# Second-layer attention of a two-layer decoder: new order of the query blocks, PSUM banks from a free list, one product on GpSimd, last head's maps turned on TensorE

## What is computed

```python
# layer 2, per head h (8 heads): two q/k maps of 128, values of 256
for i in range(S // 128):                       # 16 query blocks of 128 tokens, causal
    s = einsum('qmd,kmd->mqk', q[q0:kl], k[:kl]) * scale + bias   # m = 0, 1
    p = softmax(where(mask, s, -inf))
    a = p[0] - lam * p[1]                       # the attention map
    o = a @ v[:kl]                              # 128 x 256
o = o * rsqrt(mean(o*o) + eps) * subln_g        # RMSNorm gain, 256 values
y = (o * (1 - lambda_init) * silu(z)) @ w_out
x = LayerNorm(ALPHA * x + y)
```

## Time and profile before

| | us |
|---|---|
| median of 3 runs | 2826.72 (2821.49 to 3012.68) |
| profiled execution, its own time | 2812.25 |
| its span, slowest core (core 1) | 2810.7 |
| spans of the eight cores | 2795.7 to 2810.7 |
| PE busy in the span | 2586.8 (92%) |

### The profile page before, as it was taken

How to read it: one execution, slowest core, us unless ns; L and a number is a source line. 1 busy time by engine, 2 the same in 40 slices (tenths; PEclk the granted TensorE clock), 3 DMA queues, 4 the chain that set the end, 5 groups by cost and what they waited for, 6 DMA issues and landing times.

```text
span 2810.7 us, 70949 instructions; the slowest of 8 cores (2795.7 to 2810.7 us)
## 1 busy us (share of the span) xinstructions
PE 2586.8 (92%) x25016; PEld 1785.8 (64%) x25016; DVE 1549.8 (55%) x3656; ACT 1243.1 (44%) x3240; POOL 312.7 (11%) x645
## 2 busy tenths in 40 slices
PE   7899999999999999999999888989889898976998
PEld 4587777777777775443575648475657666663443
DVE  2544444444444443657566565656576557653766
ACT  0365555555555562533144443534353434433321
POOL 2000000000000000000112121211212122221100
PEclk9999999999999999999999999999999999998999
DMA  9222222222223269997434443444434344577753
GB/s 154 50 41 40 39 40 48 48 39 41 39 40 55 41 97 212 222 179 206 69 57 71 60 71 54 77 54 78 65 63 71 55 70 70 92 143 152 187 165 135
DMA packets 351435, 245.16 MB, mean 87 GB/s; under 512 B 279792, under 2 KB 295792, under 8 KB 346480
## 3 DMA queue, kind: packets, MB, share of 16 engines
q1 hardware_dynamic: 304736, 145.02, 23.6%
q0 software_dynamic: 45920, 92.45, 21.4%
q10 hardware_dynamic: 432, 3.15, 0.3%
HBM read 224.21 MB, written 49.15 MB: 97 GB/s over the span
## 4 chain that ended last, share of the span: by engine, by line
PE 75%; DMA 9%; DVE 8%; issue 5%; ACT 1%; SPq 1%; DVEq 0%; POOL 0%; another core or an unknown queue 0%; ACTq 0%; POOLq 0%
PE pb L525 23%; PE pb L510 23%; PE pb L338 12%; DMA M<-M 6%; PE pb L677 4%; PE pb L662 4%; PE pb L1115 4%; PE pb L1025 3%; DVE M L1089 1%; DMA A<-xs 1%; DMA x1d<-M 1%; DMA M<-x 1%; DVE M L1054 1%; DVE M L410 1%; SPq L857 1%
## 5 line engine op out<-in xcount | busy, mean ns | idle before, releaser
L665 ACT ACTIVATE M<-pb,M 128x256 bf16<-128x256 f32 (+1 forms) x1152 | 522.1, 461 | 411.0 <-PE pb L677 340.2
L525 PE MATMUL pb<-M,B 128*128 128x128 bf16 x7456 | 518.1, 222 | 0.0
L510 PE MATMUL pb<-B,M 128*128 128x512 bf16 x1848 | 505.6, 383 | 3.4 <-DVE M L773 3.3
L525 PEld LDWEIGHTS pb<-M,B 128*128 128x128 bf16 x7456 | 459.6, 99 | 16.1 <-issue 0.2
L525 PE MATMUL pb<-M,A 128*128 128x128 bf16 x6432 | 450.1, 220 | 17.3 <-DVE M L554 10.8
L510 PE MATMUL pb<-A,M 128*128 128x512 bf16 x1576 | 429.4, 386 | 5.8 <-DVE M L561 3.3
L525 PEld LDWEIGHTS pb<-M,A 128*128 128x128 bf16 x6432 | 392.5, 98 | 31.2 <-issue 19.5
L1115 PE MATMUL pb<-M 128*128 128x256 bf16 x1088 | 221.5, 288 | 114.7 <-DMA M<-M 85.4
L662 PE MATMUL pb<-M 128*128 128x256 bf16 (+1 forms) x1152 | 307.5, 267 | 8.8 <-ACT M L665 4.7
L677 PE MATMUL pb<-M 128*128 128x129 bf16 x2176 | 311.9, 221 | 1.7 <-DVE M L669 0.8
L536 DVE TENSOR_TENSOR M<-pb,M 128x512 f32<-128x512 f32 x248 | 171.1, 690 | 237.9 <-PE pb L510 99.0
(11 more groups left out here) (134 smaller groups left out, 2581.2 us busy)
## 6 DMA issues: line engine op xcount, KB each, us to landing
M<-w1s POOLq DMA_DIRECT2D x128, 256.0 KB, 5.1
M<-w0s POOLq DMA_DIRECT2D x30, 1024.0 KB, 10.4
M<-x SPq DMA_DIRECT2D x15, 1024.0 KB, 6.8
x1d<-M SPq DMA_DIRECT2D x30, 512.0 KB, 4.6
A<-x1d SPq DMA_DIRECT2D x15, 1024.0 KB, 5.3
y<-A SPq DMA_DIRECT2D x30, 512.0 KB, 3.3
gtd<-M SPq DMA_DIRECT2D x238, 64.0 KB, 2.1
B<-w1o POOLq DMA_DIRECT2D x4, 2048.0 KB, 32.4
```

The costliest lines, as they stand in the source:

```text
L510: ins = e.matmul(pb[b][:, :], lhsT=Ws.ap[:, kc * 128:kc * 128 + 128], rhs=Xs.ap[:, kc * 512:kc * 512 + 512], start=(first and kc == 0), st ...
L525: ins = e.matmul(pb[b][:, kk * 128:(kk + 1) * 128], lhsT=Xs.ap[:, kc * 512 + kk * 128:kc * 512 + kk * 128 + 128], rhs=Ws.ap[:, kc * 128:kc ...
L665: P.op("act", lambda e: e.activation(out=pt.ap[:, 0:w], in_=pb[s][:, 0:w], func=AF.Exp, bias=bs.ap[:, j * 8 + I:j * 8 + I + 1], scale=SCAL ...
```

## The change

1. Heads 0 to 5 take the query blocks in the order `MIX` (a late one, an early one, ...), with score steps due within five units less 3000 instead of six less 2000, and value steps from 7000 (was 4000) after the next unit's start. `PV_LAG` is 10000 (was 8500).
2. The accumulator bank is taken from a free list; it returns 1500 (was 1000) of emitted work after its last reader.
3. The product with the norm gain (L953 before) is issued on POOL.
4. The four DVE sums of a unit's weights are emitted 1500 apart, not together; the sums of x for the second half are placed differently in the first head.
5. `Blk.turn`: where `u == ND - 1`, the map is turned by PE matmuls against the identity into a score bank and copied back by ACT, up to eight 128x128 squares at a time, with no DMA; its values may start 3000 after.
6. In the last head the units run k0, k1, q0, q1, v0, z0, v1, z1 (the digit is the token half) instead of v0, v1, z0, z1 at the end; two of the output weights' DMAs, the first residual and two read-backs are issued at the start of v1 instead of z1 (the first read-back was at v0).
7. Residuals have eight buffers (was four), the read-back buffers move, blocks 0 to 3 are one step of the output projection, the LayerNorm rows are loaded from POOL's queue.

```diff
-                [V("A", k * 8192, 8192, F32) for k in range(3)]]
+                [V("A", 16384, 8192, F32), V("A", 40960, 8192, F32), V("M", oW + 1024, 8192, F32), V("M", oW + 18432, 8192, F32),
+                 V("A", 57344, 8192, F32), V("M", oS[0] + 8192, 8192, F32), V("M", oS[0], 8192, F32), V("M", oW + 10240, 8192, F32)]]
...
-        STEPS = [[[0, 1, 2], [3]]] * 2
+        STEPS = [[[0, 1, 2], [3]], [[0, 1, 2, 3]]]
...
-            for o, a, b in ((4, 1, 0), (1, 3, 1), (5, 3, 4), (6, 2, 5)):
-                sub_v(w[o], w[a], w[b], 0, ALU.subtract)
+            for q, (o, a, b) in enumerate(((4, 1, 0), (1, 3, 1), (5, 3, 4), (6, 2, 5))):
+                wpend[n].append(lambda o=o, a=a, b=b: sub_v(w[o], w[a], w[b], 0, ALU.subtract))
+                sc.after(1500 * q if n > 3 else 0, lambda: wpend[n].pop(0)() if wpend[n] else None)
...
-                    P.op("dve", lambda e: e.tensor_tensor(out=z3[:, st * 4:st * 4 + 4, m * 128:(m + 1) * 128], in0=b4(H.ap),
+                    P.op("pool", lambda e: e.tensor_tensor(out=z3[:, st * 4:st * 4 + 4, m * 128:(m + 1) * 128], in0=b4(H.ap),
...
                 self.t = V("M", self.p.off + 2 * w, 2 * w)
+                self.half = False
+                if u == ND - 1:
+                    self.ready = None
+                    sc.after(4000, self.turn)
+                    return
                 key = self.no % NAT
...
+            def turn(self):
+                for c in range(0, self.i + 1, 8):
+                    s, n = s_bank(), min(8, self.i + 1 - c)
+                    def f(e, s=s, n=n, c=c):
+                        for j in range(n):
+                            ins = e.transpose(pbh[s][:, j * 128:(j + 1) * 128], self.p.ap[:, (c + j) * 128:(c + j + 1) * 128], ident.ap)
+                        return ins
+                    P.op("pe", f, reads=self.p.rr(c * 128, (c + n) * 128) + ident.r, writes=bank(s))
+                    P.op("act", lambda e, s=s, n=n, c=c: e.activation(out=self.t.ap[:, c * 128:(c + n) * 128], in_=pbh[s][:, 0:n * 128], func=AF.Copy),
+                         reads=bank(s), writes=self.t.rr(c * 128, (c + n) * 128))
+                self.drop()
+                self.ready = sc.t + 3000
...
-                    self.acc = 5 + cnt["ab"] % 2
-                    cnt["ab"] += 1
+                    self.acc = accs.popleft()
...
-                sc.after(1000, lambda: cnt.update(da=cnt["da"] - 1))
+                sc.after(1500, lambda: accs.append(B.acc))
...
-        PV_LAG = 8500
-        cnt.update(da=0, ab=0)
+        PV_LAG = 10000
+        accs = deque([5, 6])
...
+        MIX = [8, 15, 9, 14, 0, 13, 1, 12, 2, 11, 3, 10, 4, 7, 5, 6]
...
-                    order = P1 + P0 if u < ND - 2 else P0 + P1
-                    DT.add(u, order, at[n], at[n + 6] - 2000, at[n + 1] + 4000, at[n + 7] + 4000)
+                order = MIX if u < ND - 2 else P0 + P1
+                DT.add(u, order, at[n], at[n + 5] - 3000, at[n + 1] + 7000, at[n + 7] + 3000)
...
+            if (u, k, p) == (ND - 1, 2, 1):
+                G.insert(0, [call(load_gp, 0, 0, 14), call(load_wo, 1, 0), call(load_res, 1, 0), call(load_wo, 1, 1), call(load_gp, 1, 0, 14)])
```

More of the change, by code:

```diff
@@ L713, in tr @@
                     P.op("dve", lambda e: e.tensor_copy(out=t.ap[:, 15 * 256:4096], in_=pbh[s][:, 0:256]), reads=bank(s), writes=t.rr(15 * 256, 4096))
-                sc.after(1800, tr)
+                sc.after(3000, tr)
                 return
@@ L804, in epi_step @@
                 else:
-                    order += [(b, i) for b in blocks[2:] for i in (0, 1)] + [(b, i) for i in (2, 3) for b in blocks]
+                    order = [(b, i) for b in blocks for i in (0, 1)] + [(b, i) for i in (2, 3) for b in blocks]
             elif li == 0 and blocks[-1] == 15:
@@ L846, in scale @@
                         x1_tr(b)
-                    if hf == 1 and b + 3 < 16 and b:
-                        sc.after(5000 * li, lambda: load_res(li, b + 3))
+                    if hf == 1 and li == 0 and 0 < b < 13:
+                        load_res(0, b + 3)
+                    if hf == 1 and li == 1 and b < 8:
+                        sc.after(5000, lambda: load_res(1, b + 8))
             for n in range(4):
@@ L872, in build_program @@
         wun = [[] for _ in range(NW)]
+        wpend = [[] for _ in range(NW)]
         neglam = misc.ap[:, 5:6]
@@ L878, in build_program @@
         dg = [V("M", oG + 1024, 512), V("M", oG + 1536, 512), V("M", oP + 2560, 512)]
-        gp = [V("A", 49152, 8192)] + [V("A", 24576 + k * 8192, 8192) for k in range(3)]
+        gp = [V("A", k * 8192, 8192) for k in (0, 1, 3, 4)]
         def load_w1(n, extra=None):
@@ L1219, in start @@
                     b = self.blocks[0]
-                    if cnt["da"] < 2 and b.ready is not None and (force or b.ready <= sc.t):
+                    if accs and b.ready is not None and (force or b.ready <= sc.t):
                         self.blocks.popleft()
-                        cnt["da"] += 1
                         self.pv.extend((c, f, t) for (c, f), t in zip(b.pv, b.tp))
@@ L1358, in build_program @@
         for u in range(1, ND):
-            for k in range(4):
+            for k in range(4 if u < ND - 1 else 2):
                 ps = (0, 1) if u == ND - 1 or (u == ND - 2 and k == 3) else (1, 0)
                 seq += [(u, k, p) for p in ps]
+        seq += [(ND - 1, k, p) for p in range(2) for k in (2, 3)]
         ucost = lambda k: 56 * mm_ns(512) if k < 2 else 224 * mm_ns(128)
@@ L1391, in build_program @@
                 flow([call(bar_fin, u - 1, p)])
[L1392 to L1398 removed]
+            if k == 2 and second and u < ND - 1:
+                order = MIX if u < ND - 2 else P0 + P1
+                DT.add(u, order, at[n], at[n + 5] - 3000, at[n + 1] + 7000, at[n + 7] + 3000)
+            if (u, k, p) == (ND - 1, 2, 0):
+                DT.add(u, range(8), at[n], at[n + 1] + 4000, at[n + 1] + 5000, at[n + 3])
+                DT.add(u, range(8, 16), at[n + 1] + 4000, end + 10000, at[n + 3], end + 25000)
             G = unit(u, k, p)
@@ L1426, in build_program, with load_late @@
                 G.insert(0, [call(diff_E, u)])
-            if u == ND - 1:
-                if k == 2 and p == 0:
-                    G.insert(0, [call(load_gp, 0, 0, 14)])
-                if k == 3 and p == 1:
-                    G.insert(0, [call(load_wo, 1, 0)] + [call(load_res, 1, q) for q in range(3)] + [call(load_wo, 1, 1)])
+            if (u, k, p) == (ND - 1, 1, 1):
+                G.insert(0, [call(wfree.extend, [slot("A", 49152 + 2048 * q) for q in range(3)])])
+            if (u, k, p) == (ND - 1, 2, 0):
+                G.insert(3, [call(sum_w1, 4 * u + 3)])
+            if (u, k, p) == (ND - 1, 2, 1):
+                G.insert(0, [call(load_gp, 0, 0, 14), call(load_wo, 1, 0), call(load_res, 1, 0), call(load_wo, 1, 1), call(load_gp, 1, 0, 14)])
             flow(sum(G, []))
+        load_res(1, 1)
         load_wo(1, 2)
-        load_gp(1, 0, 14)
-        load_wo(1, 3)
-        for dt, f in ((7000, call(load_rows, 1, "act")), (10000, call(load_res, 1, 3, "act")),
+        for dt, f in ((4000, call(load_res, 1, 2)), (8000, call(load_wo, 1, 3)), (10000, call(load_res, 1, 3)), (16000, call(load_rows, 1, "pool")),
                       (24000, call(load_gp, 2, 0, 14)), (34000, call(load_gp, 3, 0, 14))):
             sc.after(dt, f[1])
-        for n, bl in enumerate(STEPS[0] + PAIRS):
+        late = [4, 5, 6, 7]
+        def load_late(force=False):
+            if not late:
+                return
+            if not all((ND - 1, i) in done_fin for i in range(16)):
+                assert not force
+                sc.after(2000, load_late)
+                return
+            while late:
+                load_res(1, late.pop(0))
+        sc.after(30000, load_late)
+        for n, bl in enumerate(STEPS[1] + PAIRS):
+            if n == 1:
+                flow([call(finish_g, 7), call(load_late, True)])
             for I in sorted({b // 2 for b in bl}):
@@ L1443, in build_program @@
             G = epi_step(1, bl, lambda I: gp[I % 4], lambda I: h7[I])
-            for I in (4 + n,) if n < 4 else ():
+            for I in ((4, 5), (6,), (7,))[n] if n < 3 else ():
                 G.append([(0.0, lambda I=I: load_gp(I, 0, 14))])
```

44 lines of the change are left out of this document (23 added, 21 removed).

## The result

The changed kernel took 0.957 of the time of before (95% interval 0.952 to 0.963). Some executions of every kernel here show a lower granted clock on the cores of one die or both and take longer; times and ratios are of the others alone. The profiled execution took 2700.41 us with a span of 2698.8, against 2812.25 and 2810.7: 111.9 us off the span, where the prediction had 85.7. The forecast was 2741 us with a range of 2700 to 2815; 0.957 x 2826.72 is 2705, near the lower end of that range.

A forecast was written before the change was run, and what follows sets the result against it. PE, busy 2586.8 of 2810.7 us, was taken as bound by waits for chains and slow clock. Terms 61 + 3 - 4.7 + 34 - 7.6 = 85.7 us off gave 2725, plus 16 made 2741 us; range 2700 to 2815.

The forecast's parts named there:

- Heads 0 to 5: New order, windows and lag there: 11 us off each of four heads, 8.5 off heads 0 and 5, 61 us together.
- DMA transposes: Middle heads: PE's waits for transposes, at blocks 15 and 12, fall from 10.7 to 3.5 us per head.
- Score banks: Middle heads: scores stand closer, so PE's waits for score banks rise from 2.7 to 4.2 us per head.
- Slow clock: Middle heads: with the long waits mostly gone, time lost to PE's low clock falls from 7.5 to 4.5 us per head.
- Product on POOL: Gain product, 64 instructions of 128x512: 0.7 us each, bounds 0.28 and 2; no gain booked, bounds -5 and +15 us.
- Turning: Head 7 and blocks 8 to 14 of head 6: 220 squares at 0.056 us add 12.3 us; tail waits fall by 34.
- Part 4 and head 6: Last head's order: output weights land in 32.4 us, covered, nothing booked; head 6 gains 3 us from the longer lag.
- A: Heads: lead doesn't matter, landings follow DMA load and the wait moves to another block; only tail gains, 2802 us; chance 0.15.
- B: Tail gains nothing: the 22.7 us wait comes back at the first output matmul; 2766 us; chance 0.11.
- C: DVE and POOL hinder each other at the 64 products, 15 to 30 us reaching PE; 2764 us; chance 0.13.
- D: Slower: in heads 0 to 5 transposes of blocks 8 to 15 all land late, +100 us, 2927 us; chance 0.08.
- E: The change does something unsaid: seven blocks of head 6 are turned too, 4.7 us, already in the sum; no chance given.

The follow-up runs named there:

- e4: The changed kernel with the gain product back on DVE instead of POOL, nothing else changed: ratio to before 0.961 (0.957 to 0.965).
- e2: The changed kernel with before's order of query blocks in heads 0 to 5, but the new windows and lag: ratio to before 0.974 (0.970 to 0.978).
- e8: The kernel before with only the new block order, windows and lag for heads 0 to 5: ratio to before 0.966 (0.963 to 0.969).
- e6: The changed kernel without any turning on PE, all those blocks transposed by SP's DMAs: ratio to before 0.970 (0.967 to 0.973).
- Part 1 alone: Same run as e8: new block order, windows and lag for heads 0 to 5 put into the kernel before: ratio 0.966.
- the rest of the change alone: The changed kernel with before's block order, windows and lag in heads 0 to 5: ratio to before 0.975 (0.972 to 0.978).

## Why the prediction was right

Its sign, its place and its range held; it was 26 us short on the span. The time is 36 us off, not 26, since I also added the 16 us by which before's median lies above its profiled span; the changed kernel's times, 2700.41 and 2705.75 us, lie 2 and 7 us above its own. Four of its five terms for the heads were too high, so it came inside the range with 5 us to spare.

**Heads 0 to 5** (61 us forecast). From core 1 to core 1 the stretch of six and a half heads lost 151 us before and 52 after: 99. Per middle head 14.7 us were forecast and 8.0 measured:

- DMA transposes 3.5 forecast, 0 measured. This is the step that was mis-sized. I subtracted the gain in lead from the wait and added 0.5 for the rest, and so took the landing time for a constant of the block. It is none: block 15 landed in 10.6 to 12.0 us before and in 4.4 to 6.0 after, block 12 in 7.2 to 12.2 and 3.8 to 4.5. Had block 15 kept its 10.6 to 12.0 us, its map ready at 6.0 against a lead of 15.1 would have left some 2 to 3 us of wait (an estimate from these numbers), where I had 1. So the lead did about what I said, and the shorter landing did the rest; that the edit brought it was luck.
- Accumulator bank 1 forecast, none measured.
- Score banks 4.2 forecast, (10.6 + 1.7)/4 = 3.1 measured. Banks late from DVE 1.5 forecast, 1.8 measured.
- Slow clock 4.5 forecast, (522.9 - 512.4)/4 = 2.6 measured. It went down with the long waits, 5 to 7 us before; with none above 1.3 us the granted clock is 0.99.

**Product on POOL.** 0.7 us taken, 1.31 measured, inside 0.28 to 2. The Trainium skill's rule (GPSIMD Engine Reference, Elementwise), twice DVE's time, is nearer: 1.31/0.69 is 1.9. The sum didn't hang on it; DVE waited 14.6 us for products, and in e4 the four heads lose 4 us more without POOL, in one execution. POOL is idle for 97 us per head, not above 100, as a head is shorter than I forecast.

**Turning.** 220 x 0.056 us stood: their stretches lose no more than before's. The Trainium skill's 275 ns (TensorE: Matmul & The Clock Gate, Part 4: PE-mode transpose) is not borne out as a price: one turn lasts 219 ns in its record, but they follow each other at 0.056 us, and by 275 ns each the turning would have cost 60 us. ACT's copy of 1024 columns took 1.02 us, in all 28.3 us against "under 40". Tail: 53 forecast and 53.5 measured before, 19 and 19.5 after. Since the order of the last units changed, only head 6 and tail together compare strictly: 67.5 us before, 33.7 after. The split was off: turning made waits of 0.7 us at score banks, not 5, but a new 3.9 us stand at the first output bank (L339 for L774).

**Part 4 and head 6.** The weights land in 25.9 us, and no output matmul waits for them. Head 6 lost 14.2 us before and after, not 3 less.

**What the sum had no term for.** Core 1 gained 123.8 us in span. After's slowest core, 5, ends 12 us later than core 1: 8.4 us of it at the start of layer 2 (between 1024 and 1280 us of PE's work, where core 1 lost 11 to 32 us over the profiled executions), the others in heads and tail. A forecast by one core leaves this out. It also leaves out PE's waits for code, which before's last head doesn't have.

**Rivals.** A falls in its time: the wait moved to no other block, and by e2 the lead does cover a landing of 8.5 to 10.6 us. But its premise, landing times that are not the block's own, is right, and e8 doesn't speak against it. B falls by the tail's 19.5. C falls in its time by e4; the lock that it describes is in after's trace, at three products of eight. D didn't come: no transpose of the middle heads took over 8.1 us on any core. Transposes that wait on SP are real in the last head, as e6 shows. E, head 6 turned too, was so: 220 squares.

## What to carry to other kernels

A wait for a transfer can be taken away by more work before its use, by an earlier start, or by a shorter flight with less beside it. When you forecast with the first, ask whether your edit also changes the others; here the order of the blocks did. Part 1 alone gave the heads all of their gain and the rest of the change alone nearly two thirds, and together they gave no more than part 1, so before adding up the gains of two edits, ask whether they shorten the same wait. Emitting side work in small pieces (four sums of 0.7 us) took 35 us off the four heads in the old order.

A narrow item costs its chain on the other engines whatever its width: it is worth trying to lay narrow beside wide. A mean over many instructions can hide a few long ones: look at the longest too.

A DMA's place in the program is not its time. Without a semaphore it starts as soon as its queue reaches it; to hold it back, tie it to the engine's position.

## What the runs showed of the hardware

- PE can run out of code: all 43 waits of 1 us or more, up to 17.9 us, for nothing the profile names, in the last head and behind it, ended 1.2 to 1.6 us after a 16 KB packet of the instruction queue q8 had landed. The four longest (13 to 18 us, beside matmuls of 128 columns) stand where SP took 23 to 27 us to issue one read of 14 tiles of 128x256 by DMA transpose and no packet landed. On four cores of after packets did land during 29 to 32 us of issuing, so what holds them up is open. Seven pieces with gaps left 2.1 us, e4 with the whole read 3.7. The output projection of after has no such wait, with reads that take up to 40 us to issue beside matmuls of 512 columns; that PE uses its code more slowly there is argued, not shown.
- The landing time of one and the same transpose (128x16x128, block 15) was 4.4 us with no weights beside it and 10.6 to 12.0 us beside three loads of weights and the next transpose, in one execution of before.
- POOL's two-input product on 128x512 takes 1.25 to 1.59 us. A DVE instruction with both inputs in SBUF that begins while it runs stands until it ends (0.42 us became 1.49); one with an input in PSUM does not.
